# Moving buffers against the 64-byte grid of SBUF in a split-precision transformer kernel

## The reference, cut to what matters

```python
z = u @ w_in[l]                                        # 1024 -> D_IN
h = h + y @ w_o[l]
h = h + jnp.square(jax.nn.relu(v @ w_up[l])) @ w_down[l]
# layers of the second half, twice each:
gate, up = jnp.split(h @ w_in, 2, axis=-1)
return (jax.nn.silu(gate) * up) @ w_out
```

## Time and profile before

| | us |
|---|---|
| median of the three runs | 3460.66 |
| the profiled execution, first to last instruction | 3460.6 |
| PE busy in it | 3388.4 (98%) |
| PEld busy | 2652.6 (77%) |
| DVE busy | 1630.0 (47%) |
| ACT busy | 1223.9 (35%) |
| POOL busy | 432.9 (13%) |

### The profile page before, as it was taken

How to read it: one execution, slowest core, us unless ns; L and a number is a source line. 1 busy time by engine, 2 the same in 40 slices (tenths; PEclk the granted TensorE clock), 3 DMA queues, 4 the chain that set the end, 5 groups by cost and what they waited for, 6 DMA issues and landing times.

```text
span 3460.6 us, 38984 instructions
## 1 busy us (share of the span) xinstructions
PE 3388.4 (98%) x16286; PEld 2652.6 (77%) x16286; DVE 1630.0 (47%) x2132; ACT 1223.9 (35%) x1770; POOL 432.9 (13%) x338
## 2 busy tenths in 40 slices
PE   8999999999999999999999999999999999999998
PEld 6755477788888888887587888878888876878886
DVE  5555566443335635564334534475446533452233
ACT  3364465332223232224533322233323245332222
POOL 0100012121220100112011100110101210210001
PEclk9999999999999999999999999999999999999999
DMA  5412643234333334223032344333422322222221
GB/s 191 146 43 84 186 177 133 110 128 146 142 138 113 107 137 136 74 110 116 19 122 98 128 146 146 134 114 110 151 104 68 123 91 68 86 86 98 97 89 58
DMA packets 78353, 393.43 MB, mean 114 GB/s; under 512 B 8416, under 2 KB 17120, under 8 KB 45024
## 3 DMA queue, kind: packets, MB, share of 16 engines
q1 hardware_dynamic: 66048, 370.41, 30.9%
q10 hardware_dynamic: 12128, 20.52, 1.7%
HBM read 372.02 MB, written 18.87 MB: 113 GB/s over the span
## 4 chain that ended last, share of the span: by engine, by line
PE 93%; DVE 3%; ACT 2%; issue 1%; DMA 0%; POOL 0%; SPq 0%; DVEq 0%; ACTq 0%; POOLq 0%
PE pb L705 22%; PE pb L707 22%; PE pb L706 22%; PE pb L612 3%; PE pb L673 2%; PE pb L674 2%; PE pb L610 2%; PE pb L681 2%; PE pb L869 1%; PE pb L887 1%; PE pb L737 1%; PE pb L848 1%; DVE wl L2013 1%; PE pb L1200 1%; PE pb L1150 1%
## 5 line engine op out<-in xcount | busy, mean ns | idle before, releaser
L2013 DVE TENSOR_TENSOR wl<-w,wh 128x2048 fp32r<-128x2048 f32 (+3 forms) x264 | 582.2, 2205 | 898.3 <-ACT wh L1328 895.9
L705 PE MATMUL pb<-XH,wh 128*128 128x512 f32 (+1 forms) x2488 | 984.5, 396 | 2.3 <-DVE wl L2013 1.6
L707 PE MATMUL pb<-XH,wl 128*128 128x512 f32 (+1 forms) x2488 | 969.3, 390 | 0.0
L706 PE MATMUL pb<-XL,wh 128*128 128x512 f32 (+1 forms) x2488 | 969.0, 389 | 0.0
L1328 ACT ACTIVATE wh<-w 128x2048 fp32r<-128x2048 f32 (+3 forms) x264 | 471.5, 1786 | 294.3 <-PE pb L707 195.0
L705 PEld LDWEIGHTS pb<-XH,wh 128*128 128x128 f32 (+1 forms) x2488 | 465.6, 187 | 107.4 <-issue 8.2
L706 PEld LDWEIGHTS pb<-XL,wh 128*128 128x128 f32 (+1 forms) x2488 | 465.6, 187 | 101.2 <-issue 4.5
L707 PEld LDWEIGHTS pb<-XH,wl 128*128 128x128 f32 (+1 forms) x2488 | 465.2, 187 | 100.4
L2954 POOL TENSOR_TENSOR HL<-tmps,HH 128x512 fp32r<-128x512 f32 x120 | 165.8, 1384 | 1319.0 <-ACT HH L1650 1319.0
L705 PE MATMUL pb<-HH,wh 128*128 128x512 f32 x768 | 306.6, 399 | 0.0
L707 PE MATMUL pb<-HH,wl 128*128 128x512 f32 x768 | 303.7, 395 | 0.0
(11 more groups left out here) (472 smaller groups left out, 4061.4 us busy)
## 6 DMA issues: line engine op xcount, KB each, us to landing
w<-in_f_in SPq DMA_DIRECT2D x88, 1024.0 KB, 5.0
mreg<-in_mod_w SPq DMA_DIRECT2D x144, 512.0 KB, 3.6
w<-in_f_out SPq DMA_DIRECT2D x32, 1024.0 KB, 4.9
w<-in_w_up SPq DMA_DIRECT2D x16, 1024.0 KB, 5.7
w<-in_w_dn SPq DMA_DIRECT2D x16, 1024.0 KB, 5.7
w<-in_m_g SPq DMA_DIRECT2D x16, 1024.0 KB, 5.0
w<-in_f_out SPq DMA_DIRECT2D x16, 768.0 KB, 4.2
w<-in_w_rm SPq DMA_DIRECT2D x8, 1024.0 KB, 5.7
```

Source lines behind the costliest of these rows:

```text
L705: mm(dst, hi[:, cs], xh[:, k, :], start=k == 0, stop=False)
L706: mm(dst, hi[:, cs], xl[:, k, :], start=False, stop=False)
L707: x = mm(dst, lo[:, cs], xh[:, k, :], start=False, stop=fin)
L2013: tt(low[:, 0:s.cols], wslots[b % 3][:, 0:s.cols], h[:, 0:s.cols].bitcast(F32), ALU.subtract).then_inc(*DV.up(("lo", b), ("w_free", b)))
```

## The change

The six `modc` buffers, `rcol`, `cols` and `st` are placed before `hT` and no longer behind `mreg` and `tmps`. `cols` is 392 columns long and no longer 400; the columns that are left off were not used. XL, `wl0` and `wl1` are each allocated with four more columns, and the view that the kernel uses begins four columns (16 bytes) in.

```diff
         pr = sb("pr", [128, NPR])
+        modc = [sb(f"modc{i}", [128, 24]) for i in range(6)]
+        rcol = sb("rcol", [128, 4])
+        cols = sb("cols", [128, 392])
+        st = sb("st", [128, 80])
         hT = sb("hT", [128, 8, 512])
         XH = sb("XH", [128, 8, 512], F32R)
-        XL = sb("XL", [128, 8, 512], F32R)
         wslots = [sb(f"w{i}", [128, 2048]) for i in range(3)]
-        whl = [(sb(f"wh{i}", [128, 2048], F32R), sb(f"wl{i}", [128, 2048], F32R)) for i in range(2)]
+        XL = sb("XL", [128, 4100], F32R)[:, 4:4100].rearrange("p (k t) -> p k t", k=8)
+        wh0 = sb("wh0", [128, 2048], F32R)[:, :]
+        wl0 = sb("wl0", [128, 2052], F32R)[:, 4:2052]
+        wh1 = sb("wh1", [128, 2048], F32R)[:, :]
+        wl1 = sb("wl1", [128, 2052], F32R)[:, 4:2052]
+        whl = [(wh0, wl0), (wh1, wl1)]
...
-        modc = [sb(f"modc{i}", [128, 24]) for i in range(6)]
...
-        rcol = sb("rcol", [128, 4])
-        cols = sb("cols", [128, 400])
-        st = sb("st", [128, 80])
```

## The result

The changed kernel takes **3490.89 us** (median of 4 runs, 3489.93 to 3492.57), against 3462.38 us of the kernel before, run beside it (4 runs). The ratio is **1.0085**, 95% interval 1.0072 to 1.0098: slower by 0.9%. The forecast was 3493.

The account below looks back on a forecast made before the run. The prediction took PE, busy 98%, as the bound: matmul count times distance between starts. Terms of 14.4 + 16.4 + 0 + 1.5 = +32.3 us on 3460.6 gave 3493 us, 0.9% slower, range 3436 to 3523.

Parts of the forecast that it names:

- What bounds the kernel, and that only distances can act: PE is busy 98% of the span; the change keeps the matmul count and can only alter the distance between starts.
- Small buffers and cols at no cost: Placing the small buffers first and cols at 392 alters addresses only: cost 0.
- H (+6.6): In PE's matmul streams, a moving operand off the 64-byte grid costs +6.6 ns a matmul.
- S (+5.8): In PE's matmul streams, a stationary operand off the 64-byte grid costs +5.8 ns a matmul.
- XH with `wh`, twice a trio. Slot 1 stays at 0 and 0: no change: X trios: only slot 0's pairs with XH moving pay, 2488 pairs x 5.8 ns = +14.4 us.
- XL with `wl`, one charge and not two: X trios, once each: both operands off the grid pay one 6.6 ns charge, +16.4 us (bounds -28 to +31).
- H pairs at 0: H moving beside wh or wl: 2400 pairs newly have both operands off, already paid, 0 (upper bound +13.9 us).
- line 610 at +1.5: Lines 610 and 587 to 589, where weights move, mostly newly off the grid: 6.6 ns at most each, +1.5 us.
- Two charges: Rival: each operand off the grid pays its own charge in PE's pairs, +61 us, 3521 us; chance 0.17.
- Only a difference counts: Rival: PE pairs pay only when their two starts differ modulo 64, about +16 us, 3477 us; chance 0.14.
- 16 and 48 part the streams: Rival: starts at odd multiples of 16 bytes avoid read collisions in pairs with wl, -34 us, 3427 us; chance 0.22.
- Not the grid but the region: Rival: the 6 ns belong to addresses above byte 163744 or the distance between buffers; unchanged, 3461 us; chance 0.15.

Follow-up runs that it names:

- grid: The changed kernel with XL, wl0 and wl1 not shifted, all streamed buffers at one start modulo 512: 3440.80 us, ratio 0.9942 to the kernel before.
- rel32: Against grid, all four weight buffers 32 bytes further modulo 512 than XH, XL and H: 3505.78 us, ratio 1.0123 to the kernel before.
- rel64: Against grid, all four weight buffers 64 bytes further modulo 512 than XH, XL and H: 3505.05 us, ratio 1.0119 to the kernel before.
- xl16c: Against grid, XL alone starts 16 bytes in, padded so all other streamed buffers share one start modulo 512: 3475.95 us, ratio 1.0037.
- xl16: Against grid, XL alone starts 16 bytes in; its padding also put the weights 128 bytes off XH modulo 512: 3468.99 us, ratio 1.0021.
- all32: Against grid, everything from hT to BIG 32 bytes later, nothing moved against anything else: 3440.52 us, ratio 0.9935 to the kernel before.
- rel256: Against grid, all four weight buffers 256 bytes further modulo 512 than XH, XL and H, and everything 32 bytes off the 64-byte grid: 3443.13 us, ratio 0.9951.
- rel128: Against grid, all four weight buffers 128 bytes further modulo 512 than XH, XL and H: 3502.18 us, ratio 1.0114 to the kernel before.
- rel16: Against grid, all four weight buffers 16 bytes further modulo 512 than XH, XL and H: 3499.21 us, ratio 1.0100 to the kernel before.
- wl16c: Against grid, wl0 and wl1 alone start 16 bytes in, padded so all other streamed buffers share one start modulo 512: 3454.23 us, ratio 0.9974.
- xl16_wl16: Against grid, XL, wl0 and wl1 all start 16 bytes in: 3485.14 us, ratio 1.0069 to the kernel before.

## Why the prediction was right, and where it was not

**What bounds the kernel, and that only distances can act:** right. PE's busy time moved by 29.8 us, the span by 28.2, and no wait grew.

**Small buffers and cols at no cost:** right. `grid` has them and no loss. DVE's 264 instructions of line 2013 take 2207 ns on average with `wl` at its new offsets (2205 before), and DVE's busy time went from 1630.0 to 1631.7.

**The sizes H (+6.6) and S (+5.8):** right as measured, wrong as named. Before the change XH, XL and the weights all started at 448 modulo 512, and H and the extra slot at 416. What I read as "off the 64-byte grid" was "32 bytes from the partner". Both rows that I took for two effects, H moving beside grid weights and the extra slot loaded beside XH, are this one effect seen from either side; `rel32` gives 233.3 ns a matmul by it. The prediction had said that all its off-grid rows were also rows of different starts. It should have drawn a smaller confidence from that.

**"XH with `wh`, twice a trio. Slot 1 stays at 0 and 0: no change": this step failed.** The change put XH at 384 modulo 512, XL at 400, `wh0` at 416, `wl0` at 432, `wh1` at 448, `wl1` at 464 and H at 480. So slot 1, on the grid like XH, is 64 bytes off in all X pairs, and slot 0 is 32 off in all of them. With XL in step such distances cost a full trio 19 ns (`rel32`, `rel64`). XL's 16 bytes alone cost 15 (`xl16c`). Either is enough to make both slots pay, and how they share the charge here is open. By trio:

| X trios, 1244 each | forecast, ns | measured, ns |
|---|---|---|
| slot 0 | 5.8 + 5.8 + 6.6 = +18.2 | +12.7 |
| slot 1 | 6.6 | +14.4 |
| mean | +12.4 | +13.5 |

The sum came out right by luck: an overestimate of slot 0 and an underestimate of slot 1 nearly cancel, 2488 x 12.4 = 30.8 us forecast, 2488 x 13.5 = 33.6 measured by the same count. Had the distance been seen, the rows would have given the H distance, 19.1 ns, for all X trios, +47.5 us and 3508: further from the result than the wrong model. Why the changed kernel pays 693 to 695 and `rel32` and `rel64`, at the same distances, 700 is open. They differ in that XL is 16 bytes off XH, and `wl` off `wh`, in the changed kernel. The other kernels with XL shifted show the same 693 to 696 ns, so XL's start, and not the distance to the weights, may set the value there; that is not shown.

**XL with `wl`, one charge and not two:** wrong. In the changed kernel the distance behind line 710, with XL moving, is the shortest of the three on average: 229.2 ns against 233.4 and 231.8 behind lines 709 and 711. In `xl16` the pairs with XH pay as much as the pair with XL. That charges do not add holds for H: pairs with both operands "off" stayed at 232.8 ns, where two charges would have been 239.

**H pairs at 0, line 610 at +1.5:** measured -0.7 and +0.1. The size is right and the reason is not: H had been 32 bytes from its weights, and is now 16 to 64 from them.

**The rivals.** Two charges (3521): out, by the H stretches. Only a difference counts (3477): the right idea with the wrong modulus. With 64 it lets slot 1 and H with `wh0` go free, and 256 lets none go. 16 and 48 part the streams (3427): out; no float32r block of the stretches read here is faster than 226.7 ns a matmul. Not the grid but the region (3461): the region is out by `grid`. This rival also named "the distance between buffers", which was right, and then took it that shifts of 16 to 48 bytes would leave that alone, which was wrong. The prediction read the 16-byte cachelines of the Trainium skill, "SBUF — State Buffer", section "Door 1: The DMA port swizzle", as making all starts equally good. `all32` agrees that a common shift of 32 bytes is free (226.7 ns in `grid` and in `all32`); the rule names no distance between two streams, and that is where the 6 ns are.

**The rule weighed against S.** The Trainium skill, same page, section "Who interferes with whom", has two independent read ports of PE. The runs disagree: from `grid` to `rel64` XH, XL and H keep one common start, the stationary ones move 64 bytes away from it, and the pace goes from 226.7 to 233.3 ns. The two streams do feel each other. The 226.7 ns of the free case against 215.5 for bf16 may be a further part of this; no run tried it.

**What would have shown it sooner.** The prediction's own test said that slot 1 should keep lines 705 and 707 at 227. The blocks of the timeline refuted it at once, although the total was within 2.1 us of the forecast. A right total is no proof of the steps.

The best version seen is `grid` or `all32`, 22 us below the kernel before and 50 below the changed one; the two don't differ by more than their intervals.

## What to carry to other kernels

When two buffers stream at once into one engine, check their starts against each other and not against a grid: here all streamed buffers, high and low parts alike, at one start modulo 256 bytes were worth 0.6% of the kernel, and 0.9% was lost by giving each its own. An effect that every row shows together with a second difference is not yet known by its cause; an experiment that moves everything by the same amount, and one that moves one side by another amount, tell the two apart in one go. Padding placed to shift one buffer shifts all that stand behind it, so print the start of every buffer modulo 512 before believing that only one thing changed.

## What the runs showed that was not expected

- A stream of 128x512 float32r matmuls has a fast pace of 226.7 ns and slow ones of 231 to 233.3 ns each, at the same granted clock and with no wait in the profile. Where high and low parts are in step, the distance between the moving and the stationary operand decides: equal or 256 bytes apart is fast (`grid`, `all32`, `rel256`), 32, 64 or 128 apart slow (`rel32`, `rel64`, `rel128`), and 16 apart slow nearly everywhere (`rel16`).
- At a distance of 16 bytes either pace can hold for a whole stretch: 11.14 and 10.88 us for 48 matmuls in `wl16c` (low weights alone off), 11.20 and 10.88 in `rel16` (all weights off).
- XL alone out of step slows the whole trio (695.9 ns in `xl16c`), not only the matmul that reads it. With XL off, trios are slow even where every pair is at a free distance (695.9 ns in slot 1 of `xl16_wl16`); why is open.
